# A two-layer hybrid backbone in fp32 on one core: four conditioning slots go to the layer 1 FFN, attention D runs in column blocks, and three smaller edits

## The reference

```python
mod_x = s_c @ w_mod[l] + b_mod[l]      # six vectors of 1024; likewise mod_c for the context
px = (h_x * (1 + ca_x) + sa_x) @ w_in[l]
mix_x = concat(window attention A, global attention B,
               gated linear recurrence (HGRN2) C, neighbourhood attention D)
h_x = layer_norm(ALPHA * h_x + ga_x * (mix_x @ w_out[l]))
f_x = conv_ffn(h_x * (1 + cf_x) + sf_x)
h_x = layer_norm(ALPHA * h_x + gf_x * f_x)
# conv_ffn: u = h @ w_up (5632 columns); 3-tap convolution over tokens, both halves;
#           (silu(a) * v) @ w_down
```

## Time and profile before

| | |
|---|---|
| median of 3 runs | 1996.57 us (1995.75 to 1996.68) |
| the profiled execution | 2004.46 us, its span 2002.6 us |
| busy PE, DVE, ACT, POOL | 1895.2, 1307.8, 898.8, 926.5 us |
| mean granted TensorE clock | 0.975 |
| FFN up, layer 0 and layer 1 | about 599 to 996 us and 1626 to 1867 us |
| attention, layer 0 and layer 1 | about 390 to 525 us and 1458 to 1565 us |

### The profile page before, as it was taken

The page is one execution under the profiler, slowest core; times in us unless marked ns, Lnnn a source line. Parts: engine busy times, 40 slices in busy tenths (PEclk is TensorE's granted clock), DMA queues, the critical chain, the costliest instruction groups (busy, mean ns, idle before and its releaser), DMA issues.

```text
span 2002.6 us, 32824 instructions
## 1 busy us (share of the span) xinstructions
PE 1895.2 (95%) x12510; PEld 1606.9 (80%) x12510; DVE 1307.8 (65%) x2566; ACT 898.8 (45%) x1917; POOL 926.5 (46%) x770
## 2 busy tenths in 40 slices
PE   6899799999999999999999999998999989999997
PEld 4788798867778888878888878898877778778786
DVE  3248999676585999999744263999776842222545
ACT  3224588577533222222343342565567543333442
POOL 3145467111345345553353335756432545775643
PEclk9999899999999999999999999999999999999999
DMA  8563000210111333233221121101130212222321
GB/s 349 210 241 114 26 23 22 96 49 2 43 63 43 127 126 118 93 118 117 103 74 63 53 105 64 59 28 43 43 122 1 88 47 98 105 84 91 120 98 71
DMA packets 27372, 177.31 MB, mean 89 GB/s; under 512 B 2896, under 2 KB 4048, under 8 KB 8144
## 3 DMA queue, kind: packets, MB, share of 16 engines
q1 hardware_dynamic: 22976, 158.16, 21.8%
q10 hardware_dynamic: 4240, 17.04, 2.1%
HBM read 171.00 MB, written 4.19 MB: 87 GB/s over the span
## 4 chain that ended last, share of the span: by engine, by line
PE 69%; DVE 13%; POOL 6%; issue 5%; ACT 3%; DMA 2%; SPq 0%; DVEq 0%; ACTq 0%; POOLq 0%
PE PS L1270 20%; PE PS L1165 18%; PE PS L881 9%; PE PS L875 4%; PE PS L1127 3%; PE PS L1105 3%; POOL WS L2412 3%; PE PS L1014 2%; DMA WR<-in_weights 2%; PE PS L1089 2%; DVE W L1687 2%; DVE U L1922 1%; PE PS L1095 1%; PE PS L810 1%; DVE W L2031 1%
## 5 line engine op out<-in xcount | busy, mean ns | idle before, releaser
L1270 PE MATMUL PS<-XH,WS 128*128 128x512 f32 x2016 | 543.6, 356 | 4.6 <-POOL WS L2412 4.6
L1270 PEld LDWEIGHTS PS<-XH,WS 128*128 128x128 f32 x2016 | 360.5, 190 | 60.2 <-issue 4.9
L1270 PE MATMUL PS<-XL,WS 128*128 128x512 f32 x1008 | 358.6, 356 | 0.0
L2412 POOL TENSOR_TENSOR WS<-WR,WS 128x1024 fp32r<-128x1024 f32 x88 | 215.5, 2450 | 289.1 <-ACT WS L1558 288.7
L1623 ACT ACTIVATE W<-PS,PR 128x768 f32<-128x768 f32 (+1 forms) x88 | 78.0, 886 | 424.6 <-PE PS L1270 360.7
L2241 DVE SCALAR_TENSOR_TENSOR W<-PS,PR,W 128x511 f32<-128x511 f32 (+1 forms) x132 | 83.0, 657 | 208.2 <-ACT W L1623 208.2
L1270 PEld LDWEIGHTS PS<-XL,WS 128*128 128x128 f32 x1008 | 191.5, 190 | 26.6
L881 PE MATMUL PS<-EU,XH 128*128 128x256 f32 x624 | 190.1, 305 | 5.6 <-issue 4.6
L2349 POOL TENSOR_TENSOR WL<-WR,EU 128x512 fp32r<-128x512 f32 x96 | 128.8, 1368 | 126.0 <-ACT EU L1327 126.0
L881 PE MATMUL PS<-EU,HL 128*128 128x256 f32 x624 | 182.4, 292 | 0.0
L881 PE MATMUL PS<-WL,XH 128*128 128x256 f32 x624 | 182.3, 292 | 0.0
(11 more groups left out here) (220 smaller groups left out, 4259.1 us busy)
## 6 DMA issues: line engine op xcount, KB each, us to landing
WR<-in_weights SPq DMA_DIRECT2D x128, 1024.0 KB, 4.8
U<-in_weights SPq DMA_DIRECT2D x16, 1024.0 KB, 7.5
U<-in_bias ACTq DMA_DIRECT2D x2, 1792.0 KB, 9.4
H<-in_x SPq DMA_DIRECT2D x1, 2048.0 KB, 7.8
H<-in_x ACTq DMA_DIRECT2D x1, 2048.0 KB, 14.5
U<-in_ln_rows ACTq DMA_DIRECT2D x2, 1024.0 KB, 4.8
WR<-in_weights SPq DMA_DIRECT2D x4, 512.0 KB, 3.5
kept<-H ACTq DMA_DIRECT2D x4, 512.0 KB, 2.6
```

What stands on the lines that cost most here:

```text
L1270: mm = pe.matmul(PS[u.pos][:, lo:hi], w[:, part, k, :], src[:, k, lo:hi], start=(k == 0 and src is xh3 and part == 0), stop=(k == KT - 1 a ...
L2412: pool.tensor_tensor(ws5[:, u.c % 2, 1], half_slot(u), ws5[:, u.c % 2, 0], ALU.subtract).then_inc(w_low, 1)
```

## The change

- **Slots.** `mods_behind` now has the layer as an argument. Layer 0's FFN does slots 5 to 19, behind `j` = 2 to 20 without 6, 10, 14 and 18; layer 1's FFN does slots 20 to 23 behind `j` = 2, 4, 15 and 17. The weight stream follows.
- **Rows.** `restore` is split into `rescale` and `shift_row`. In the FFN one of them stands behind each `j` from 5: until 16 in layer 0, until 12 in layer 1.
- **First down tile.** Its entry is now in `EW`, beside the up input, and `high_tiles` for it stands before `gate(FT - 1)` and before the wait for the last up unit.
- **Attention D.** Queries, keys and values are ordered by blocks of 16 columns x 8 rows. A tile of queries sees its own block and the neighbours: two or three local blocks where it saw four. ACT writes Q and K of D in that order; for V, it stores two pairs of tiles to DRAM (`vrows`) as they come and, behind the bias load at the end of the scan, loads four tiles back in the new order; PE waits for them before D's values. DVE writes D's outputs back in token order. The bias table is re-cut to 7 x 128 columns a head.
- **Scan.** The two products with the state of one head each become one of 128 columns.

```diff
+BIAS_AT = (0, 2, 2, 5)
+BIAS_COLS = 7 * P
+LATE = 20
-def mods_behind(j):
-    return int(1 < j <= 25 - EARLY)
+def mods_behind(l, j):
+    if l == 0:
+        return int(1 < j <= 20 and j not in (6, 10, 14, 18))
+    return int(j in (2, 4, 15, 17))
...
-                   [whole(t[:, e * ENTRY:(e + 1) * ENTRY]) for t in (XH, XL, EW) for e in range(2)])
+                   [whole(t[:, e * ENTRY:(e + 1) * ENTRY]) for t, e in ((EW, 0), (XH, 0), (XH, 1), (XL, 0), (XL, 1), (EW, 1))])
...
-                        elif g == "A":
+                        elif g in "AD":
                             a.lo, a.hi = max(0, t - 1), min(NLT, t + 2)
...
+                        pe.matmul(ob[:, 0:P], QE[u.g % 2][:, 0:P], SS[:, u.d, u.b, :], start=True, stop=False)
                         for hh in range(2):
-                            oh = ob[:, hh * 64:(hh + 1) * 64]
-                            pe.matmul(oh, QE[u.g % 2][:, 0:P], SS[:, u.d, u.b, hh * 64:(hh + 1) * 64],
-                                      start=True, stop=False)
-                            mm = pe.matmul(oh, AT[u.d][u.no % 2][:, hh, :], vslice[:, hh * 64:(hh + 1) * 64],
-                                           start=False, stop=True)
+                            mm = pe.matmul(ob[:, hh * 64:(hh + 1) * 64], AT[u.d][u.no % 2][:, hh, :],
+                                           vslice[:, hh * 64:(hh + 1) * 64], start=False, stop=(hh == 1))
...
+                    if a.grp == "D":
+                        pe.wait_ge(v_turned, 16 * NLT * (l + 1))
...
+                            if j.slot in (QD, KD) and j.b == 0:
+                                to = to.rearrange("p (m r c) -> p r m c", m=NLT, r=NA_ROWS)
+                                of = of.rearrange("p (r m c) -> p r m c", m=NLT, r=NA_ROWS)
...
+                    if j.slot == VD and 2 * j.a < NLT:
+                        act.wait_ge(job_act, j.after[0])
+                        if l > 0:
+                            act.wait_ge(v_turned, 16 * NLT * l)
+                        act.dma_start(vrows[2 * j.a * P:(2 * j.a + 2) * P, :].rearrange("(i p) c -> p i c", p=P),
+                                      vv["D"][:, 2 * j.a:2 * j.a + 2, :]).then_inc(v_stored, 16)
...
                 act.dma_start(biasv, bias_d[l]).then_inc(bias_in, 16)
+                act.wait_ge(v_stored, 16 * (NLT // 2) * (l + 1))
+                vblocks = vrows.rearrange("(r m c) d -> m r c d", r=NA_ROWS, m=NLT)
+                for t in range(NLT):
+                    act.dma_start(vv["D"][:, t, :], vblocks[t]).then_inc(v_turned, 16)
...
                     if u is real[-1]:
+                        high_tiles(2 * l + 1, k_tiles[2 * l + 1][0])
                         gate(FT - 1)
                     act.wait_ge(up_sum, u.c + 1)
-                    if u is real[-1]:
-                        high_tiles(2 * l + 1, k_tiles[2 * l + 1][0])
...
-                    if 0 <= j - 8 < restored[2 * l]:
-                        restore(2 * l, j - 8)
+                    if 0 <= j - 5 < 2 * restored[2 * l]:
+                        (rescale, shift_row)[(j - 5) % 2](2 * l, (j - 5) // 2)
```

More of the change, by code:

```diff
@@ L133, in uses @@
         u += [("out", l, n, g) for n in range(2) for g in range(KT // KDN)]
-        nxt = list(range(EARLY, 24)) if l + 1 < DEPTH else []
+        nxt = list(range(EARLY, LATE) if l + 1 < DEPTH else range(LATE, 24))
         for j in range(FT):
             u.append(("up", l, j, 0))
-            for _ in range(mods_behind(j)):
-                if nxt:
-                    u.append(("mod", l + 1, nxt.pop(0), 0))
+            for _ in range(mods_behind(l, j)):
+                u.append(("mod", 1, nxt.pop(0), 0))
         assert not nxt
@@ L170, with hybrid_backbone @@
 ENTRY = 2 * TOK + 2 * 512
-def hybrid_backbone(nc, weights, x, ctx_in, consts, masks, params, bias_d, ln_rows, kept, out):
+def hybrid_backbone(nc, weights, x, ctx_in, consts, masks, params, bias_d, ln_rows, kept, vrows, out):
     f32, u8 = mybir.dt.float32, mybir.dt.uint8
@@ L621, in hybrid_backbone @@
                 u = Job()
-                u.kind, u.l, u.j, u.key = "mod", key[1] - 1, key[2], key
+                u.kind, u.l, u.j, u.key = "mod", int(key[2] >= LATE), key[2], key
                 ups.append(u)
@@ L740, in mods_done @@
         def mods_done(l):
-            return 24 * (l + 1) + (EARLY if has_ctx(l) else 0)
+            return 24 * (l + 1) + (EARLY if has_ctx(l) else LATE - 24)
         def half_slot(u):
@@ L2091, in outputs @@
                     roots = RB[a.quad % 2].rearrange("p (k t) -> p k t", k=2)
-                    dve.tensor_tensor(x3[:, k0:k0 + 2, a.t * P:(a.t + 1) * P],
-                                      bank(7)[:, 0:256].rearrange("p (k t) -> p k t", k=2), roots,
-                                      ALU.mult).then_inc(o_norm, 1)
+                    if a.grp == "D" and a.t < NLT:
+                        dst = x3[:, k0:k0 + 2, 0:SEQ].rearrange("p k (r m c) -> p k r m c", r=NA_ROWS, m=NLT)[:, :, :, a.t, :]
+                        sums, roots = [w.rearrange("p (k r c) -> p k r c", k=2, r=NA_ROWS)
+                                       for w in (bank(7)[:, 0:256], RB[a.quad % 2])]
+                    else:
+                        dst = x3[:, k0:k0 + 2, a.t * P:(a.t + 1) * P]
+                        sums = bank(7)[:, 0:256].rearrange("p (k t) -> p k t", k=2)
+                    dve.tensor_tensor(dst, sums, roots, ALU.mult).then_inc(o_norm, 1)
                 def scores(a):
@@ L2386, in attention @@
                     if l > 0 and 0 <= n - 2 < restored[2 * l - 1]:
-                        restore(2 * l - 1, n - 2)
+                        rescale(2 * l - 1, n - 2)
+                        shift_row(2 * l - 1, n - 2)
                     if n in (split_at, split_at + 1):
@@ L2413, in low_part, with rescale @@
                                    ALU.subtract).then_inc(w_low, 1)
-            def restore(m, t):
+            def rescale(m, t):
                 if t == 0:
@@ L2532 @@
     rpb = A(na_rpb)
-    bias = np.full((DEPTH, 2, GRID_W, HEADS, BIAS_ROWS, GRID_W), NEG, f)
-    for col in range(GRID_W):
-        c0 = min(max(col - NA_COLS // 2, 0), GRID_W - NA_COLS)
-        o0 = c0 - col + NA_COLS - 1
-        for a in range(2):
-            bias[:, a, col, :, :, c0:c0 + NA_COLS] = rpb[:, :, 1 - a:1 - a + BIAS_ROWS, o0:o0 + NA_COLS]
-    bias = bias.reshape(DEPTH, P, HEADS, BIAS_ROWS * GRID_W)
+    bias = np.full((DEPTH, NA_ROWS, BLOCK, HEADS, 7, NA_ROWS, BLOCK), NEG, f)
+    for m in (0, 1, NLT - 1):
+        lo, hi = max(0, m - 1), min(NLT, m + 2)
+        for c in range(BLOCK):
+            col = m * BLOCK + c
+            c0 = min(max(col - NA_COLS // 2, 0), GRID_W - NA_COLS)
+            for n in range(lo, hi):
+                for e in range(BLOCK):
+                    key = n * BLOCK + e
+                    if c0 <= key < c0 + NA_COLS:
+                        for r in range(NA_ROWS):
+                            bias[:, r, c, :, BIAS_AT[m] + n - lo, :, e] = (
+                                rpb[:, :, NA_ROWS - 1 - r:2 * NA_ROWS - 1 - r, key - col + NA_COLS - 1])
+    bias = bias.reshape(DEPTH, P, HEADS, BIAS_COLS)
     ln_rows = np.concatenate([A(ln_g), A(ln_b)], -1).reshape(2 * DEPTH, 2 * D_MODEL)
@@ L2548 @@
     kept = nc.dram_tensor("kept", (SEQ, D_MODEL), mybir.dt.float32, kind="Internal").ap()
-    hybrid_backbone(nc, *aps, kept, out)
+    vrows = nc.dram_tensor("vrows", (SEQ, 256), mybir.dt.float32, kind="Internal").ap()
+    hybrid_backbone(nc, *aps, kept, vrows, out)
     r = run_bass_kernel_spmd(nc, [{f"in_{k}": v for k, v in arrays.items()}], core_ids=[0])
```

30 lines of the change are left out of this document (19 added, 11 removed).

## The result

The changed kernel takes 2009.3 us (median of 5 runs, 2005.1 to 2012.6), the kernel before 1996.7 beside it: ratio 1.0057 between the means, 95% interval 1.0035 to 1.0078. One of the five runs of the kernel before took 2482.5 us and is left out of the ratio. The forecast was 1983.4 and faster, with a range up to 1998; the time lies outside it, and the sign is the other one. The profiled execution of the changed kernel took 2010.19 us (span 2008.3), 5.7 more than the profiled one of before.

A forecast was written before the change was run, and what follows sets the result against it. PE, busy nearly throughout, was taken to bound the kernel. Gains of 45.2 less 32 lost gave 13.2 us less: 2004.46 to 1991.3 profiled, and 7.9 lower for the median, 1983.4; 8 in 10 range 1959 to 1998.

The forecast's parts named there:

- V through DRAM: Start of attention: four loads on ACT's queue take 1.8 us against 1.0 of room; loss 1.6 (0.5 to 4).
- attention D: Both layers' D: shorter units run at A's pace on PE; gain 18 us, lower bound 12, both layers 19.1.
- four slots in layer 1: Layer 1's FFN: PE waits 6.1 us for DVE's macs, 8.0 a slot in all; 32 us lost (8 to 41).
- layer 0's FFN, transposes too: One POOL pass per j cuts PE's waits for macs, gain 12.5 (7.5 to 15); four slots fewer save 1.8.
- state product: Scan: one product of 128 columns instead of two saves 3.5 us (0 to 8.8); DVE nearly full there.
- layer 1's restores: Layer 1's FFN: each single restore pass fits before the next low weights; gain 4 us (0 to 4).
- first down tile: Both FFNs: tile ready early removes PE's wait and slow products at the first down product; gain 7 (3.5 to 7.8).
- rival 2: Layer 1's slots cost more through late weight loads, 12.8 each, 51 us: 2002.6; decides from 11.3 a slot; chance 0.08.
- layout of the 16 passes: Layer 1's slot: POOL holds DVE's macs, ending near 1662.4 when PE wants them at 1656.3; wait 6.1 us.
- rival 1: Layer 1's FFN: the slots' macs hide on DVE, cost 8 instead of 32: 1959; chance 0.15.
- rival 3: Attention D doesn't get shorter, or V comes late; the 18 us go: 2001; chance 0.07, wholly or half.
- rival 4: Layer 1's slots: clock stays low longer behind each wait, 5 us instead of 1.4, 14 more: 1998; chance 0.05.

The follow-up runs named there:

- 3: Changed kernel with V's four loads issued one each at attention units 4, 6, 8 and 10: 1997.4 us, ratio 0.999 to the kernel before.
- 12: Changed kernel with V in one load (eight column-block stores a layer) and the bias load at the 5th attention unit: 2000.1 us, ratio 1.0011.
- 5: Changed kernel with all of attention D as before, V straight from SBUF: 2009.0 us, ratio 1.0065 to the kernel before.
- 1: Changed kernel with all 19 slots in layer 0's FFN again, none in layer 1's: 1972.1 us, ratio 0.9866 to the kernel before.
- 7: Changed kernel with the scan's state product in two halves of 64 columns again: 2009.7 us, ratio 1.0052 to the kernel before.
- 4: Changed kernel with both restoring passes of a token tile behind one j again, from j 8: 2016.4 us, ratio 1.0092.
- 8: Changed kernel with the first down tile in XH again, behind the wait for the last unit: 2013.1 us, ratio 1.007.
- 9: Changed kernel with the bias load alone moved to attention unit 4: 2004.3 us, ratio 1.0036 to the kernel before.
- 6: Changed kernel with V stored in column blocks (eight stores a layer) and loaded back in one load, same place: 2009.9 us, ratio 1.006.

## Why the prediction was wrong, step by step

Between the profiled executions it said 13.2 us less and 5.7 more were measured, a miss of 18.9:

| step | said | measured | from |
|---|---|---|---|
| V through DRAM | +1.6 | +10.0 | first row of the first table; 3 and 12 take it off |
| attention D | -18 | -13.8 | second row; 5 |
| four slots in layer 1 | +32 | +36.4 | 1 |
| layer 0's FFN, transposes too | -14.3 | -12.3 | 14.6 less the wait of 2.27 that counts below |
| state product | -3.5 | about -3 | 7, not shown |
| layer 1's restores | -4 | -3.4 to -4.7 | 4; before against 1, each up to the first down wait |
| first down tile | -7 | -5.3 to -6.7 | 8; the last rows of before and after |

1. **V's way was the step that failed**: 10.0 us measured against 1.6, six times as much and past its upper bound of 4. It set 1.8 us for four issues, at 0.45 to 0.53 each, against 1.0 of room. The price came from the issues of other loads, and the issues behind V's were taken to stay as short as before. Shown by 3, 9, 6 and 12 is a higher price, 0.58 to 0.81 us each (the program's first 1.18), and stalls behind them, in layer 1 of 2.54 and 1.63 us where 0.45 and 0.53 stood. PE's slow clock came on top.
2. **D was mis-sized.** The change took 24 transposes and 48 products with V out of the stretch (92 and 192 instead of 116 and 240 in the groups of before and of 3). The busy time of the two groups fell by 2.8 and 3.1 us and that of the scores by 2.1: 8.0 us of PE in layer 0. Of these 0.5 is the slow clock at the end of before's stretch (experiment 5 has 16.2 for 16.7), which leaves 7.5; 7.0 came. The groups of before and then of 3, each over its own D stretch:

```profile
L1127 PE MATMUL PS<-W,U 128*64 128x128 f32 x240 | 16.7, 283 | 0.0
L1105 PE MATMUL PS<-CN,W 128*128 128x128 f32 x116 | 15.6, 278 | 1.6 <-ACT W L1538 1.5
L1089 PE MATMUL PS<-U 64*128 64x512 f32 x28 | 7.9, 641 | 0.0
```

```profile
L1133 PE MATMUL PS<-W,U 128*64 128x128 f32 x192 | 13.6, 280 | 0.0
L1109 PE MATMUL PS<-CN,W 128*128 128x128 f32 x92 | 12.8, 280 | 1.5 <-ACT W L1560 1.4
...
L1093 PE MATMUL PS<-U 64*128 64x384 f32 (+1 forms) x28 | 5.8, 489 | 0.0
```

   I had used the pace of A instead, 9.6 a layer. Scores of D in the changed kernel, layer 0, show it: from 482.99 to 490.49 and on to 498.35 are the two pairs of middle tiles, 7.5 and 7.9 us and not 7.22.

```profile
482.99 0.56 DVE L2144 CUSTOM_DVE_ANT_0 W<-PS,U 128x384 f32<-128x384 f32 x1 [0.49 <-PE PS L1093]
...
490.49 0.56 DVE L2144 CUSTOM_DVE_ANT_0 W<-PS,U 128x384 f32<-128x384 f32 x1 [0.49 <-PE PS L1093]
...
498.35 0.42 DVE L2144 CUSTOM_DVE_ANT_0 W<-PS,U 128x256 f32<-128x256 f32 x1 [0.28 <-PE PS L1093]
```

   The count of the products that go could have been made before the run.
3. **The slots were right in mechanism, and in part by luck in the number.** The wait is 6.4 us instead of 6.1 and the slow clock costs 1.44 (the mean of the four blocks above) instead of 1.4. What I left out is that the transposes themselves stand right behind the wait and run slow too: 1.09 us instead of 0.44. 6.4 + 1.1 + 1.4 = 8.9 of the 9.1. POOL's passes did fall otherwise than laid out: the load behind the slot, which rival 2 has, moved the second low weights by 2.7 us. The same five POOL instructions still fell on the macs, so their end hardly moved. The change is slower, as rival 2 said, but not by its price: 9.1 us a slot are under its 11.3. The prediction's sentence that a pass with one SBUF input is not held is wrong for the two tensor-scalar passes: 2.09 and 1.37 us beside POOL at 1624.46, and 0.34 without it. Its layout of the 16 passes had held these two as well, and needs no change.
4. **The halved restores were right**; of rival 1 (the macs hide), rival 3 (D no shorter) and rival 4 (a clock low for a whole `j`) none came: the clock is at 1.00 again in the second of the windows above.
5. **The offset from profile to median didn't carry over.** Between the medians the loss is 12.6 us (11.3 between the means), between the two profiled executions 5.7. The prediction took 7.9 us off the profiled one for the median; the changed kernel's profiled execution lies 0.9 above its median. This goes with the clock. In the 59 runs of the kernel before beside the experiments, the nine shortest, 1989.8 to 1993.3 us, have a mean granted clock of 0.984 or 0.985, and the nine longest, 2002.7 to 2007.3, have 0.974 to 0.977. The profiled 2004.46 was one of 0.975; the changed kernel's profiled execution has 0.970, and so has its median run. One such slow stretch is placed, 1.5 us at the end of layer 0's D (49.88; experiment 5 has 48.39). The changed kernel's profiled execution has the same one, so the gain of D in the table stands. Where the other slow stretches of the longer runs lie, and why they come in some runs only, is not shown.

The sign was wrong because a net gain of 13 was the difference of 45 and 32, and the three large misses (V 8.4, D 4.2 and the slots 4.4 us) all lay on one side.

## What to carry to other kernels

Put work into an idle engine only after placing its result in the consumer's order: the same four slots cost 9.1 us each with PE's transposes behind the same `j`, and 2.4 when PE turns the sums one `j` later. Move no load to the front of an engine's first urgent instruction: the issue is time of that engine, and it can grow with what stands in the queue already; spread over the loop, V's four loads cost nothing that can be seen. When a part shortens a stretch that PE sets, count the instructions that go, and don't take the pace of a similar stretch.

## What the runs showed of the hardware

An issue of a load on ACT's queue took 0.35 to 0.53 us plain, and 0.58 to 0.81 for 128 rows of 1 KB picked in blocks of 16 (the first of the program 1.17 to 1.18). It took up to 4.44 when 4.4 MB had been issued just ahead (bias, V in one load, and H) and 2.54 behind 2.3 MB (bias, and V in four loads), but 0.53 behind 3.8 MB (bias and H). A DVE tensor-scalar pass of 256 columns took 0.34 us alone, and the two of layer 1's first slot took 2.09 and 1.37 beside POOL. After a wait of 6.4 us PE's granted clock was 0.54, about the lower of its two levels (1.2 of 2.4 GHz), for 3 us and 1.00 from then on; after one of 1.8 us it fell in the kernel before (24 products in 7.34 us), and in experiment 8 it did not (5.72). Behind two waits of 1.22 and 0.83 us, the same in fourteen kernels, it was 0.50 in six and 1.00 in eight.
